# Differential attention: the maxima of an item taken ahead of the finish of the item before it, and the scores made one item further ahead

## The reference, cut to what matters

```python
def diff_attn_core(q1, q2, k1, k2, v, lam):
    scale = DIFF_QK_DIM ** -0.5
    s1 = jnp.einsum('bqhd,bkhd->bhqk', q1, k1).astype(jnp.float32) * scale
    s2 = jnp.einsum('bqhd,bkhd->bhqk', q2, k2).astype(jnp.float32) * scale
    a = jax.nn.softmax(s1, axis=-1) - lam * jax.nn.softmax(s2, axis=-1)
    return jnp.einsum('bhqk,bkhe->bqhe', a.astype(v.dtype), v)
```

## Time and profile before

| | us |
|---|---|
| median of 3 runs | 2058.43 |
| their range | 2058.36 to 2059.71 |
| the profiled execution | 2058.17 |
| its span in the trace | 2056.0 |
| busy TensorE / VectorE / ScalarE | 1911.4 / 1243.5 / 1069.3 |

### The profile page before, as it was taken

How to read it: one execution, slowest core, us unless ns; L and a number is a source line. 1 busy time by engine, 2 the same in 40 slices (tenths; PEclk the granted TensorE clock), 3 DMA queues, 4 the chain that set the end, 5 groups by cost and what they waited for, 6 DMA issues and landing times.

```text
span 2056.0 us, 25790 instructions
## 1 busy us (share of the span) xinstructions
PE 1911.4 (93%) x10392; PEld 1579.1 (77%) x10392; DVE 1243.5 (60%) x1379; ACT 1069.3 (52%) x1368; POOL 43.6 (2%) x38
## 2 busy tenths in 40 slices
PE   6999889979999998898887999999999999999995
PEld 4889456868888786788567788888888888888784
DVE  3241751452222334442654889898989898888886
ACT  4232642352222224433534677677777777676764
POOL 0000000000000000000000020000000000000000
PEclk9999885889999999899967899999999999999997
DMA  8211633212222222212802899998989998989894
GB/s 336 103 62 63 226 145 121 73 49 105 83 103 102 82 103 82 89 62 103 307 22 82 319 350 368 338 368 343 366 342 364 344 362 346 360 343 343 336 339 163
DMA packets 61530, 441.87 MB, mean 215 GB/s; under 512 B 6836, under 2 KB 6964, under 8 KB 8288
## 3 DMA queue, kind: packets, MB, share of 16 engines
q1 hardware_dynamic: 60032, 436.23, 56.3%
q10 hardware_dynamic: 1120, 3.28, 0.4%
q0 software_dynamic: 256, 0.66, 0.1%
HBM read 439.10 MB, written 1.05 MB: 214 GB/s over the span
## 4 chain that ended last, share of the span: by engine, by line
PE 84%; DVE 10%; ACT 3%; DMA 2%; issue 1%; SPq 0%; DVEq 0%; ACTq 0%
PE psum L1446 72%; DMA raw<-units 2%; PE psum L1782 2%; PE psum L1658 1%; PE psum L1664 1%; DVE act_lo L1088 1%; PE psum L1641 1%; PE psum L1825 1%; DVE row_max L1168 1%; PE psum L1463 1%; PE psum L1798 1%; ACT probs L773 1%; DVE states L1199 1%; PE psum L1469 1%; DVE y_mix L1237 1%
## 5 line engine op out<-in xcount | busy, mean ns | idle before, releaser
L1331 DVE TENSOR_TENSOR w_lo<-raw,w_hi 128x2048 fp32r<-128x2048 f32 x136 | 311.0, 2289 | 52.3 <-ACT w_hi L922 51.6
L922 ACT ACTIVATE w_hi<-raw 128x2048 fp32r<-128x2048 f32 x136 | 260.8, 1919 | 109.0 <-PE psum L1446 106.4
L1024 DVE TENSOR_TENSOR w_lo<-raw,w_hi 128x1024 fp32r<-128x1024 f32 x130 | 153.3, 1221 | 197.9 <-ACT w_hi L628 197.9
L1446 PE MATMUL psum<-w_hi,xt_hi 128*128 128x512 f32 x596 | 234.2, 393 | 2.7 <-DVE xt_lo L1336 2.7
L1446 PE MATMUL psum<-w_hi,xt_lo 128*128 128x512 f32 x596 | 233.4, 392 | 0.0
L1446 PE MATMUL psum<-w_lo,xt_hi 128*128 128x512 f32 x596 | 233.2, 391 | 0.0
L1331 DVE TENSOR_TENSOR w_lo<-raw_more,w_hi 128x2048 fp32r<-128x2048 f32 x90 | 206.0, 2290 | 35.7 <-ACT w_hi L922 35.3
L628 ACT ACTIVATE w_hi<-raw 128x1024 fp32r<-128x1024 f32 x130 | 130.2, 1051 | 157.2 <-PE psum L1446 151.6
L922 ACT ACTIVATE w_hi<-raw_more 128x2048 fp32r<-128x2048 f32 x90 | 172.8, 1920 | 75.4 <-PE psum L1446 75.4
L1446 PE MATMUL psum<-act_hi,w_hi 128*128 128x512 f32 (+1 forms) x544 | 208.8, 384 | 2.1 <-DVE act_lo L1088 1.9
L1446 PE MATMUL psum<-act_lo,w_hi 128*128 128x512 f32 (+1 forms) x544 | 207.6, 382 | 0.0
(11 more groups left out here) (260 smaller groups left out, 3636.1 us busy)
## 6 DMA issues: line engine op xcount, KB each, us to landing
raw<-units SPq DMA_DIRECT2D x295, 1024.0 KB, 4.9
raw_more<-units SPq DMA_DIRECT2D x120, 1024.0 KB, 4.9
X<-ctx_in ACTq DMA_DIRECT2D x1, 1024.0 KB, 16.6
X<-x_in ACTq DMA_DIRECT2D x1, 1024.0 KB, 23.3
out<-X SPq DMA_DIRECT2D x1, 1024.0 KB, 4.1
const<-const_in ACTq DMA_DIRECT2D x1, 520.0 KB, 9.6
rope<-rope_in POOLq DMA_DIRECT2D x2, 256.0 KB, 5.6
wsm<-wsm_in ACTq DMA_DIRECT2D x1, 288.0 KB, 26.9
```

What stands on the lines that cost most here:

```text
L922: act.activation(w_place(m)[0], raw_place(m), ACT.Copy).then_inc(esem("w_high"), 1)
L1024: ins = dve.tensor_tensor(w_lo[:, i % RING, part], raw[:, i % RING, part], w_hi[:, i % RING, part].bitcast(F32), ALU.subtract)
L1331: dve.tensor_tensor(lo, raw_place(m), hi.bitcast(F32), ALU.subtract).then_inc(esem("w_ready"), 1)
L1446: ins = pe.matmul(dst, lhs(a), rhs(b), start=first and n == 0, stop=last and n == 2)
```

## The change

Two orders are turned round, in both layers; no instruction is added or removed.

```diff
@@ psum_jobs
         n = len(attn_items(l))
+        out += [("S", l, 0, 0), ("S", l, 0, 1)]
         for i in range(n + 2):
-            if i < n:
-                out += [("S", l, i, 0), ("S", l, i, 1)]
+            if i + 1 < n:
+                out += [("S", l, i + 1, 0), ("S", l, i + 1, 1)]
@@ VectorE, attention(l)
             for i in range(n + 1):
+                if i < n:
+                    b, keys = i % 2, n_keys(items[i][1])
+                    for j in range(2):
+                        wait_filled(dve, ("S", l, i, j))
+                        ins = dve.tensor_reduce(row_max[:, b, j:j + 1], bank(("S", l, i, j))[:, 0:keys], X_AXIS, ALU.max)
+                    link(ins)
+                    dve.tensor_scalar(neg_max[:, b, :], row_max[:, b, :], -QK ** -0.5, None, ALU.mult).then_inc(
+                        sem(f"neg_max{l}"), 1)
                 if i >= 1:
                     b, keys = (i - 1) % 2, n_keys(items[i - 1][1])
...
-                if i < n:
...
@@ TensorE, attention(l)
+            scores(0)
             for i in range(n + 2):
-                if i < n:
...
+                if i + 1 < n:
+                    scores(i + 1)
                 beside_item(l, "att", 2 * i)
```

More of the change, by code:

```diff
@@ L1575, in attention, with scores @@
                     wait_copied(pe, ("K", l, u, g))
-            for i in range(n + 2):
-                if i < n:
[L1578 to L1585, removed]
+            def scores(i):
+                h, t = items[i]
+                keys = n_keys(t)
+                for j in range(2):
+                    key = ("S", l, i, j)
+                    wait_emptied(pe, key)
+                    r = slice(j * QK, (j + 1) * QK)
+                    pe.matmul(bank(key)[:, 0:keys], qT[r, h, t * P:(t + 1) * P], kT[r, h, 0:keys], start=True,
+                              stop=True).then_inc(filled, 1)
+            scores(0)
+            for i in range(n + 2):
+                if i + 1 < n:
+                    scores(i + 1)
                 beside_item(l, "att", 2 * i)
```

## The result

| | before | after |
|---|---|---|
| median, us | 2059.07 of 4 runs | 2088.59 of 4 runs |
| their range | 2058.36 to 2062.63 | 2086.50 to 2090.77 |
| the profiled execution | 2058.17 | 2090.77 |
| its span | 2056.0 | 2088.7 |

The ratio is 1.014, with a 95% interval of 1.0122 to 1.0158. The change costs 29.5 us, where I had forecast 10. That is outside my range (2059 to 2077), and on the number of rival B, TensorE at half clock for most of layer 1 (2088).

A forecast was written before the change was run, and what follows sets the result against it. TensorE, busy 93% of the span, was taken as the overall bound. From 2058.17, -4.8 (layer 0) + 10.0 (layer 1) + 5 (clock) gave 2068.4, stated as 2068.5 us; range 2059 to 2077.

The forecast's parts named there:

- rival B: Layer 1: TensorE at half clock for most of it, +5 us for each of five turns, 2088 us; chance 0.12.
- Layer 0, forecast -4.8: Layer 0's attention: 1.9 gained early, 3.1 late, 0.2 lost between; 4.8 us gained, bounds 4 and 6.
- forecast 1.9: Layer 0, items 0 to 4: the finish moves behind, so item 2's exponentials start 1.9 us earlier.
- forecast 3.1: Layer 0, items 8 to 15: exponentials 4.26 us apart against 4.71, seven spacings, 3.1 us gained.
- Layer 1, first items: Start of layer 1's attention: exponentials of item 1 earlier by 1.7 us, of item 2 by 3.0.
- Layer 1, the loop: Layer 1, items 3 to 7: serial loop round three engines through the shared banks, 8.38 us a turn against 5.85.
- second score tile 0.53 (half of 1010.27 to 1011.33): Term of layer 1's 8.38 us turn: the second score tile takes half of the pair's time, 0.53 us.
- my +10.0: Layer 1's end: last `mod` waits for item 7's exponentials and delays a load; +10.0 us, bounds +9 and +11.
- The clock: Layer 1: TensorE's waits bring half clock; half of five or six turns lose 1.9 us: +5, bounds 0 and +11.
- Rival A: Layer 1: serial loop without clock loss, 2063.4 us, between 2061 and 2065.5; chance 0.22.
- Rival C: Layer 1: bank wait does not bind, turns stay at 5.85 us, both layers gain, 2050.4 us; chance 0.08.
- A gain of layer 0 is passed on: Behind layer 0: loads follow TensorE within reach, so its 4.8 us gain reaches the end.

The follow-up runs named there:

- the repeated kernel: Second measurement of both orders changed in layer 0 only, with separate PSUM banks for its attention results there, against before: 2056.92 us, ratio 0.9976 to 0.9995.

## Why the prediction was right or wrong

**Direction and mechanism: right; the size: wrong.** Layer 0 gains, layer 1 loses more, over a ring from the bank of S(i) back to the exponentials of the next item. The kernels with one layer each bear out both halves.

**Layer 0, forecast -4.8: -3.7 in the profile of the change, -5.1 to -5.3 in those four other kernels that have the same layer 0, partly by luck.** The exponentials of item 2 came 6.48 after the first, against 8.33 before: 1.85, forecast 1.9. The spacing of items 11 to 15 is 4.38, forecast 4.26: `mod` starts 0.93 behind the exponentials and not 0.82. So items 8 to 15 gained 2.5 us, forecast 3.1, and of the first 1.9 us 1.4 were left at item 8 in the kernel with layer 0 alone, forecast 1.7. What makes up for both is 1.3 us behind the exponentials of item 15 (9.3 us before, 8.0 in that kernel), which my sum doesn't have: 16 matmuls of O, in part at half clock before, took 3.46 us there and 2.07 in that kernel. What the profile of the change lacks is in items 3 to 6: 5.43, 5.43 and 4.21 us apart, where the kernel with layer 0 alone has 5.43, 4.55 and 3.50. There TensorE was at full speed until `mod` waited 2.80 us for the exponentials to free its bank, and the granted clock was 0.50 from item 3 to item 5. The bank wait costs clock in layer 0 too.

**Layer 1, first items: right, then cut short.** Item 1 came 5.74 after item 0, against 7.48: 1.7 early, as forecast. Item 2 was 2.3 early where I had 3.0. Item 3 should have been 2.0 early and was 2.2 late: from 987 us on TensorE was at half clock.

**Layer 1, the loop: mis-sized by 0.5 us a turn.** At full clock it is 8.87 to 8.92, not 8.38. The failed term is "second score tile 0.53 (half of 1010.27 to 1011.33)". Measured in place of it: 1.06, from 998.75 to 999.81. The rest of the sum holds: 8.38 + 0.53 = 8.91. That is also where the 12.2 us for the loop, against my +10.0, come from in the main: 2.0 of the difference arise from item 3 to item 7.

**The clock: the step that failed.** I put +5, "if half of them lose 1.9 us", with +11 as the upper bound. Measured: 19.9 us. I took the price of one wait from the earlier trace rows, where TensorE ran 3.7 us at half clock and came back. I then bounded six turns by six such events. In the ring of layer 1 a wait of up to 2.7 us comes in every turn. What I treated as six separate events was here one lasting state. That the bank wait holds it is shown (with the wait filled the clock is 1.00 from item 3 on, with own banks 1.00 from item 4 on); why one wait of 1.82 in layer 0 was followed by a return and these were not is open. Its price is not a count of waits but the whole of TensorE's work in the turn once more, which was rival B's way to count: 8.38 + 5.06 = 13.44, measured 13.49 (996.14 to 1009.63). I gave B 0.12. That the two are so close is partly luck. With the score tile at its measured 1.06 the doubled sum is 8.91 + 5.59 = 14.50; the turn was 1.0 shorter, because its steps took less than twice as long (a `mod` 1.87 in place of 2.00) and its second small `modc` instruction was missing. B's total of 2088 is lucky too: it had 25 us for the clock, where 19.9 were measured, and 10 for the loop, where it was 12.2; and the profiled execution had 4.3 us more outside the two attentions. The upper bound of the clock term should have been B's, +25, and the range should have reached 2088.
The row that I held against B was the clock of 0.92 in layer 1 before. It was no evidence: before, TensorE itself waited little in that stage, 3.7 us in five waits from 975 to 1014 us, and the long waits were VectorE's. The row to ask was how long TensorE itself stands still, and by my own sum that was 2.65 in each turn.
The Trainium skill's "TensorE: Matmul & The Clock Gate", section "A second HAM failure mode: psum-queue depth-cycling", names this pattern, a swing between the levels when TensorE pauses between its groups. The trace agrees that such pauses cost the clock, but shows less of a swing: 0.66 over 74.65 us, with one return in seven turns.

**The rest.** Rival A (2063.4) has no clock loss. With the loop at 12.2 it would have been 2065.6; the kernel with 2 unused matmuls a turn, where that loss is gone, gave 2069.1. The 3.5 us between them are about as much as layer 0's gain loses on its way to the end, below; that it is the same isn't shown. Rival C fell with the loop. It would also have been wrong in size: with its condition met (own banks), layer 1 still lost 7.4. I had not seen that the finish, once behind the maxima, gates PT and so the next `modx`: 2.2 of the 7.4 us. "A gain of layer 0 is passed on" holds only in part: 5.3 us in the profile, 4.0 at the end of the same execution, 0.8 in the median of ten; and the whole change is only 0.3 us faster than layer 1 alone (2088.59 and 2088.88). About 1 us of it goes in the stretch right behind, where the profiles of all kernels with a changed layer 0 and no short half-clock stretch have 687.3 to 687.6 us between the layers in place of 686.5. The rest is open.

## What to carry to other kernels

Before an instruction is moved ahead on TensorE, look up whose PSUM bank it gets, and who frees that bank: as many results a turn as there are banks means that moving ahead by one item is waiting for the next reader. If the answer is a wait of TensorE that comes back in every turn, price it at both clock levels: once as a loop at full clock, and once with all of TensorE's work in the loop at half clock, and let the range reach the second. An order that helps where VectorE waits for ScalarE (layer 0) hurts where it waits for TensorE (layer 1), so apply it by stage: here layer 0 alone with banks of its own is faster than before and than the change, though by little: 2055.3 and 2056.9, against 2058.6 and 2058.4 for before in the same sessions.

## What the runs showed of the hardware

**More work made it faster.** 24 unused matmuls in the waits took 18.5 us off the median, and 12 took 19.5 us off. What went up with it is the granted clock: 0.66 between first and last exponentials of the change, 0.94 with either.

**Two score tiles together cost as much as one.** Each uses 64 rows of the array. Released together the pair takes 1.13 us; released 0.66 apart, 1.79, of which 1.06 are behind the second weight load (998.75 to 999.81). Half of a pair's time was therefore no price for one of them. At half clock the pair took 2.08 released together and 2.74 released 0.67 apart. The Trainium skill has the rule in "TensorE: Matmul & The Clock Gate", section "Why this matters for your kernels": matmuls with few rows, each in its own group of rows, run at the same time, while one alone takes as long as a full one. The trace agrees: the pair took 1.13, one of it 1.06, and an unused matmul, which uses all 128 rows, 0.92. I hadn't put that beside my half.

**Short stretches at half clock amid steady matrix products, in some executions and not in others.** Windows of the same stretch, ahead of all changed code, of before and of after:

```profile
100.00:150.00 50.00, 50.00 (x304) 41.88 (x304) 20.90 (x27) 17.46 (x25) 0.00 (x0) 1.00 0.15 50
```
```profile
100.00:150.00 50.00, 50.00 (x280) 41.22 (x279) 20.89 (x27) 17.45 (x25) 0.00 (x0) 0.93 0.14 47
```

TensorE is busy in all of the 50 us in both, and yet the clock is 0.93 in one (7% of 50 us is 3.5), and layer 0 started 2.9 us later there. The profile of the change has more of these between the layers, the repeated kernel had the one at the start (208.3 us to its first exponentials, 687.5 between the layers), its first profile the reverse (205.4 and 691.5). Between these two profiles of one kernel they went with 2.9 us at the start and 4.0 between the layers; why they come I can't say. Here a gain of 3 us took eleven runs to be seen, against 29 of before.
